# A second home for the first half of each odd expert's w1 in a streamed mixture of experts

## The reference

```python
def _moe(h, w_router, b_router, w1, b1, w2, b2):
    logits = (xt @ w_router + b_router).astype(jnp.float32)
    top_val, top_idx = lax.top_k(logits, TOP_K)            # 4 of 32
    top_w = jax.nn.softmax(top_val, axis=-1)
    gates = ...                                            # 288 x 32, zero where not chosen
    for e in range(N_EXPERTS):
        gu = xt @ w1[e] + b1[e]                            # w1[e]: 1024 x 2048, 8.39 MB
        gate = jnp.minimum(gu[:, :D_FF], SWIGLU_LIMIT)
        up = jnp.clip(gu[:, D_FF:], -SWIGLU_LIMIT, SWIGLU_LIMIT)
        act = (up + 1) * (gate * jax.nn.sigmoid(SWIGLU_ALPHA * gate))
        out = out + gates[:, e:e + 1] * (act @ w2[e] + b2[e])   # w2[e]: 1024 x 1024, 4.19 MB
```

## Time and profile before

| | |
|---|---|
| median of 3 runs | 1116.15 us |
| the profiled execution | 1115.64 us, its span 1113.7 us |
| PE busy | 1053.9 us, 95% of the span |
| DVE, ACT, POOL busy | 393.3, 238.8, 15.5 us |
| DMA | 421.78 MB, mean 379 GB/s over the span |
| mean granted TensorE clock | 0.99 |

### The profile page before, as it was taken

The page is one execution under the profiler, slowest core; times in us unless marked ns, Lnnn a source line. Parts: engine busy times, 40 slices in busy tenths (PEclk is TensorE's granted clock), DMA queues, the critical chain, the costliest instruction groups (busy, mean ns, idle before and its releaser), DMA issues.

```text
span 1113.7 us, 14012 instructions
## 1 busy us (share of the span) xinstructions
PE 1053.9 (95%) x5312; PEld 434.0 (39%) x5313; DVE 393.3 (35%) x694; ACT 238.8 (21%) x473; POOL 15.5 (1%) x27
## 2 busy tenths in 40 slices
PE   8989999999999998999999999999999999999996
PEld 7766454333333333333333333333333333333332
DVE  7683347333333332333333323322322232223326
ACT  3233214221111121222222222111221222111212
POOL 1003000000000000000000000000000000000000
PEclk9989899999999999999999999999999999999998
DMA  9750235999999999999999999999999999999992
GB/s 319 280 227 1 86 155 210 430 428 430 427 430 428 429 428 434 433 432 432 433 433 432 433 432 430 432 431 430 432 431 433 432 433 432 433 425 429 428 428 88
DMA packets 28554, 421.78 MB, mean 379 GB/s; under 512 B 5326, under 2 KB 5966, under 8 KB 11547
## 3 DMA queue, kind: packets, MB, share of 16 engines
q1 hardware_dynamic: 28346, 420.93, 89.4%
q10 hardware_dynamic: 192, 0.66, 0.2%
HBM read 420.11 MB, written 1.46 MB: 379 GB/s over the span
## 4 chain that ended last, share of the span: by engine, by line
PE 51%; DMA 40%; DVE 7%; ACT 1%; issue 1%; SPq 0%; DVEq 0%; ACTq 0%
DMA ring<-in_w_dram 39%; PE ps L880 27%; PE ps L906 8%; PE ps L610 4%; PE ps L727 3%; PE ps L943 1%; DVE area L1598 1%; PE ps L861 1%; PE ps L589 1%; DVE area L1576 1%; DVE area L1572 1%; DVE area L1579 1%; DVE area L1573 1%; PE ps L674 1%; PE ps L872 1%
## 5 line engine op out<-in xcount | busy, mean ns | idle before, releaser
L880 PE MATMUL ps<-ring,area 128*64 128x512 f32 x2048 | 458.1, 597 | 20.3 <-DMA ring<-in_w_dram 20.3
L880 PEld LDWEIGHTS ps<-ring,area 128*64 128x64 f32 x2048 | 142.5, 137 | 291.1 <-issue 245.0
L906 PE MATMUL ps<-ring,area 128*64 128x512 f32 x992 | 224.9, 595 | 0.0
L1598 DVE TENSOR_TENSOR area<-area,ps 128x1024 f32<-128x1024 f32 (+1 forms) x96 | 116.5, 1214 | 55.4 <-PE ps L943 55.4
L1572 DVE TENSOR_SCALAR area<-ps 128x512 f32<-128x512 f32 x31 | 21.4, 692 | 278.5 <-PE ps L880 278.5
L906 PEld LDWEIGHTS ps<-ring,area 128*64 128x64 f32 x992 | 67.5, 136 | 120.7 <-issue 118.3
L1220 ACT ACTIVATE area<-area 128x512 f32<-128x512 f32 x31 | 19.5, 629 | 411.1 <-DVE area L1572 411.1
L1564 DVE SCALAR_TENSOR_TENSOR y_sb<-ps,gcol,y_sb 64x512 fp32r<-64x512 f32 x62 | 46.5, 750 | 98.5 <-ACT y_sb L1182 98.0
L943 PE MATMUL ps<-y_sb,giveT 128*128 128x512 f32 x192 | 69.4, 443 | 11.9 <-DVE area L1598 11.9
L852 PE MATMUL ps<-area 128*64 128x512 bf16 x558 | 66.1, 382 | 0.0
L1182 ACT ACTIVATE y_sb<-ps,gcol 64x512 fp32r<-64x512 f32 x62 | 42.4, 683 | 92.4 <-PE ps L906 91.6
(11 more groups left out here) (238 smaller groups left out, 647.4 us busy)
## 6 DMA issues: line engine op xcount, KB each, us to landing
ring<-in_w_dram SPq DMA_DIRECT2D x60, 4096.0 KB, 20.1
ring<-in_w_dram SPq DMA_DIRECT2D x72, 2048.0 KB, 16.2
area<-in_w_o_dram SPq DMA_DIRECT2D x1, 4096.0 KB, 13.3
area<-in_w_in_dram SPq DMA_DIRECT2D x1, 2560.0 KB, 16.3
area<-in_w_in_dram SPq DMA_DIRECT2D x1, 2336.0 KB, 9.5
area<-in_w_in_dram SPq DMA_DIRECT2D x1, 2048.0 KB, 20.5
lnb<-in_ln_g_dram SPq DMA_DIRECT2D x3, 512.0 KB, 10.4
lnb<-in_ln_b_dram SPq DMA_DIRECT2D x3, 512.0 KB, 11.7
```

The costliest lines, as they stand in the source:

```text
L880: last = mm(ps_gu[g * BLK:(g + 1) * BLK, c, :], x[:, spot(k), :], half_of(w, c, g), start=False, stop=(k == KT - 1))
L906: last = mm(ps_y[g * BLK:(g + 1) * BLK, :], hT[:, c, h, :], w2_t[:, h, c, g * 512:(g + 1) * 512], start=False, stop=(h == 1 and c == 3))
L1598: v.tensor_tensor(acc, acc, src[0:n, :, :], ALU.add).then_inc(done, 1)
```

## The change

The first half of w1 (slots 0 and 1) gets a second home, `late`, two slots wide. Even passes use the ring's slots 0 and 1, odd passes use `late`. The rest of an expert (slots 2 to 5) stays in the ring. To make room, tensors of attention and routing that are dead by then lie inside `late`; those that still live while it fills (`chosen`, `shifted`, `n_more` and so on) move to the end of `area`; `gx` lies on `g_sb`; ln2's gain and bias lie on `rows`, which are free once the rows have been split, so these two loads go out after the first eight passes' loads. PE's loop runs over two passes. SP issues in the order in which buffers come free: the first half of pass p + 2, then the rest of pass p + 1. The table `passes` now holds the first 32 passes as constants, and DVE counts only the further ones, rounded to an even number of passes.

```diff
@@ tensors @@
-        tokT = sb("tokT", [P, KT, TOK])
-        lnb = sb("lnb", [P, 2, D])
-        uext = sb("uext", [P, 4, UW])
+        late = sb("late", [P, 2 * SLOT])
...
+        uext = carve(late, 4 * UW).rearrange("p (g n) -> p g n", g=4)
+        attT = carve(late, 4 * TOK).rearrange("p (k t) -> p k t", k=4)
+        lnb = carve(late, 2 * D).rearrange("p (i n) -> p i n", i=2)
+        assert used[0] >= SLOT
+        tokT = carve(late, KT * TOK).rearrange("p (k t) -> p k t", k=KT)
...
+        gx = g_sb
+        last_giveT = rows[:, 0, 0:TOKP]
+        last_y = rows[:, 0, TOKP:TOKP + D // 2]
+        ln2 = rows[:, 1:3, :]
@@ SyncE @@
             sp.wait_ge(ln_done, 2 * NT)
-            sp.dma_start(lnb[:, 0, :], ln2_g[0].partition_broadcast(P)).then_inc(ln_in[2], 16)
-            sp.dma_start(lnb[:, 1, :], ln2_b[0].partition_broadcast(P)).then_inc(ln_in[2], 16)
...
+            sp.dma_start(late[:, 0:SLOT], w1_part(1, 0)).then_inc(w_in_odd[0], 16)
+            sp.wait_ge(router_ps, 2)
+            sp.dma_start(late[:, SLOT:2 * SLOT], w1_part(1, 1)).then_inc(w_in_odd[1], 16)
+
+            def first_half(i, e, odd, wide):
+
+                base, ready, free = (late[:, :], w_in_odd, odd_free) if odd else \
+                    (ring[:, 0:2, :].rearrange("p s n -> p (s n)"), w_in_slot, slot_free)
+                if wide:
+                    sp.wait_ge(free[0], i + 1)
+                    sp.wait_ge(free[1], i + 1)
+                    sp.dma_start(base, w1_v[col(e), 0].rearrange("e p n -> p (e n)")).then_inc(ready[0], 16)
+                    return
...
+            def two_passes(i, wide):
+
+                even = expert_of(sp, 2 * i + 2)
+                first_half(i, even, False, wide)
+                rest(2 * i + 1, expert_of(sp, 2 * i + 1), wide)
+                first_half(i, expert_of(sp, 2 * i + 3), True, wide)
+                rest(2 * i + 2, even, wide)
+
+            end_wide = last_wide(sp)
+            with sp.Fori(0, WIDE_PAIR) as i:
+                two_passes(i, False)
+            sp.wait_ge(split_ready, NT)
+            sp.dma_start(ln2[:, 0, :], ln2_g[0].partition_broadcast(P)).then_inc(ln_in[2], 16)
+            sp.dma_start(ln2[:, 1, :], ln2_b[0].partition_broadcast(P)).then_inc(ln_in[2], 16)
+            with sp.Fori(WIDE_PAIR, end_wide) as i:
+                two_passes(i, True)
+            two_passes(end_wide, False)
+            rest(2 * end_wide + 3, expert_of(sp, 2 * end_wide + 3), False)
@@ TensorE @@
-                    if k % 2 == 0:
+                    if k % 2 == 0 and k < 4:
+                        pe.wait_ge((w_in_odd if odd else w_in_slot)[k // 2], 16 * (i + 1))
+                    elif k % 2 == 0:
                         pe.wait_ge(w_in_slot[k // 2], 16 * (e + 1))
...
-            with pe.Fori(0, end) as e:
-                expert(e)
+            with pe.Fori(0, end_wide + 1) as i:
+                expert(2 * i, i, False)
+                expert(2 * i + 1, i, True)
+            expert(2 * end_wide + 2, end_wide + 1, False)
@@ ScalarE @@
                 act.wait_ge(x_rows, e + 1)
+                act.wait_ge(sig_ready, e + 1)
+                act.wait_ge(prod_ready, e + 1)
                 copy(gx, ps[:, 2, :]).then_inc(gx_ready, 1)
```

More of the change, by code:

```diff
@@ L35 @@
 TAKEN = -3.0e38
+ROUND = 8388608.0
 BLK = 64
@@ L145, in encoder_kernel @@
         assert BP + 3 * F // 2 + D <= KT * IN
+        flat = area[:, BP + 3 * F // 2:BP + 3 * F // 2 + D]
+        shifted, kept, expo, weighed = (flat[:, i * NT * NE:(i + 1) * NT * NE].rearrange("p (t e) -> p t e", t=NT)
+                                        for i in range(4))
+        n_more, incl, earlier_of = (flat[:, (4 * NT + i) * NE:(4 * NT + i + 1) * NE] for i in range(3))
+        chosen = flat[:, (4 * NT + 3) * NE:(5 * NT + 3) * NE].rearrange("p (t e) -> p t e", t=NT)
         used = [0]
@@ L234, in encoder_kernel @@
         w_in_slot = [sem(f"w_slot{s}") for s in range(NSLOT)]
+        w_in_odd = [sem(f"w_odd{s}") for s in range(2)]
+        odd_free = [sem(f"odd_free{s}") for s in range(2)]
         bias_in = sem("bias_in")
@@ new lines, in _ @@
+            sp.wait_ge(router_ps, 2)
[8 more added lines that the diff above has]
+                    return
+                for s in range(2):
+                    sp.wait_ge(free[s], i + 1)
+                    sp.dma_start(base[:, s * SLOT:(s + 1) * SLOT], w1_part(col(e), s).rearrange("e p n -> p (e n)"))\
+                        .then_inc(ready[s], 16)
@@ new lines, in rest @@
+            def rest(p, e, wide):
+                for s in (2, 4) if wide else (2, 3, 4, 5):
+                    if wide:
+                        src = w1_v[col(e), 1] if s == 2 else w2_whole[col(e)]
+                        dst = ring[:, s:s + 2, :]
+                        sp.wait_ge(slot_free[s + 1], p)
+                    else:
+                        src = w1_part(col(e), s) if s < 4 else w2_v[col(e), s - 4]
+                        dst = ring[:, s, :]
+                    sp.wait_ge(slot_free[s], p)
+                    sp.dma_start(dst, src.rearrange("e p n -> p (e n)")).then_inc(w_in_slot[s], 16)
@@ L556, in _ @@
             pool.wait_ge(ln_in[2], 32)
[L557 to L560, removed]
+            with pool.Fori(WIDE_PAIR, last_wide(pool)) as i:
+                for first, p in ((w_in_slot, 2 * i + 1), (w_in_odd, 2 * i + 2)):
+                    pool.wait_ge(first[0], 16 * (i + 2))
+                    pool.sem_inc(first[1], 16)
+                    for s in (2, 4):
+                        pool.wait_ge(w_in_slot[s], 16 * (p + 1))
+                        pool.sem_inc(w_in_slot[s + 1], 16)
             pool.wait_ge(scaled, 1)
-            nc.gpsimd.tensor_tensor(out_acc[:, 0, :], out_acc[:, 0, :], lnb[:, 1, :], ALU.add).then_inc(result[0], 1)
+            nc.gpsimd.tensor_tensor(out_acc[:, 0, :], out_acc[:, 0, :], ln2[:, 1, :], ALU.add).then_inc(result[0], 1)
         @block.tensor
@@ L882, in up_products @@
                     if k % 2 == 1 and k < KT - 1:
-                        last.then_inc(slot_free[k // 2], 1)
+                        last.then_inc((odd_free if odd and k < 4 else slot_free)[k // 2], 1)
                     if k == 1:
@@ L954, in _, with expert @@
             pe.wait_ge(bias_ready, 1)
-            def expert(e, last=False):
+            def expert(e, i, odd, last=False):
                 pe.wait_ge(xT_ready, e + 1)
                 pe.wait_ge(sel_ready, e + 1)
-                up_products(xT, e)
+                up_products(xT, e, i, odd)
                 if last:
@@ L1026, in add_last @@
                 last.then_inc(sum_ps[t], 1)
-            expert(end, last=True)
+            expert(2 * end_wide + 3, end_wide + 1, True, last=True)
         @block.scalar
@@ L1659, in _ @@
             dve.wait_ge(scaled, 2)
-            v.tensor_tensor(halves(out_acc[:, 1, :]), ps_sum[1], halves(lnb[:, 1, :]), ALU.add).then_inc(result[1], 1)
+            v.tensor_tensor(halves(out_acc[:, 1, :]), ps_sum[1], halves(ln2[:, 1, :]), ALU.add).then_inc(result[1], 1)
             centre(2)
@@ L1664, in _ @@
             dve.wait_ge(norm_ready, NT + 3)
-            v.scalar_tensor_tensor(row, row, rstd[0:TS, 2:3], lnb[0:TS, 1, :], ALU.mult, ALU.add).then_inc(result[2], 1)
+            v.scalar_tensor_tensor(row, row, rstd[0:TS, 2:3], ln2[0:TS, 1, :], ALU.mult, ALU.add).then_inc(result[2], 1)
 _INS = ['x_prompt', 'x_sample', 'cache_k', 'cache_v', 'cache_kidx', 'state_pool', 'ln0_g', 'ln0_b', 'w_in', 'w_o',
```

97 lines of the change are left out of this document (41 added, 56 removed).

## The result

The changed kernel takes 1117.53 us, median of 17 runs (1116.05 to 1119.95), beside 1115.86 for the kernel before in as many runs. The ratio is 1.0018, its 95% interval 1.001 to 1.0025: slower by 1.7 us, clear of no change by the interval, but under the 2.2 us that the prediction took as the line to slower. The forecast was 1118.0. The profiled execution took 1117.42 us with a span of 1115.5, 1.8 longer than before.

A forecast was written before the change was run, and what follows sets the result against it. The weight stream was taken as the bound until pass 28's second half of w1 lands, then TensorE's own pace. 1115.64 + 3.34 - 1.60 + 0.15 = 1117.53, at the median 1118.0 us; own range 1117.0 to 1118.7, overall 1112 to 1123.5.

The forecast's parts named there:

- the line to slower: Verdict threshold: about 0.2%, 2.2 us, from no change, so a time above 1118.4 would count as slower.
- What bounds the end: Last passes: landing of pass 28's second half of w1, plus TensorE's own work from there, plus 1.60 us.
- R28: Pass 28's loads of slots 2 to 5; their half was forecast to land near 995.8, before just ahead of 992.39.
- The prefetch frees only pass 31's waits: Stream's end: only pass 31's loads come 9.7 us earlier, removing its waits of 1.07 and 0.53, gain 1.60 us.
- The ln2 loads: Two loads moved behind pass 8's weights: delay later second halves and the end by 3.34 us (bounds 2.4 and 3.4).
- The doubled loop: TensorE's loop body over two passes: some 570 instructions, three or four 16 KB packets, priced at nothing in the sum.
- The routing arithmetic: VectorE's extra tiny operations before pass_cols, ready about 175.2 instead of 174.47: +0.15 us (bounds 0 and 0.7).
- Pass 9: TensorE waits about 5.8 us instead of 2.14, perhaps with a longer low clock, hidden by 1.18 us a pass.
- (1): Weight stream: the whole 9.7 us of the prefetch come through, 1109.9 us; chance 0.14.
- (2): ln2 loads in the stream: cost nothing visible, as the same 4 KB is read 128 times, 1114.7 us; chance 0.10.
- (3): Wide part of the stream: runs at the narrow part's rate, 428 not 432, adding 5.4 us, 1123.4; chance 0.08.
- (4): Doubled TensorE loop: instructions fetched at each turn, about 1134 to 1138, taken as 1136 us; chance 0.06.

The follow-up runs named there:

- The experiment that takes the lead out ahead of R: Changed kernel with ln2 loads last and, from pass 9, slots 2 to 5 of the next pass loaded before the following pass's first half; ratio to before 0.9944.
- plain rows: Changed kernel with ln2 loads after all weights, plus two 512 KB loads of different w1 rows in their old place behind pass 8's loads; ratio to before 1.0020.
- the loop of five: Kernel before with only TensorE's loop written over five passes (6 turns); ratio to before 1.0001.
- the experiments on ln2: Changed kernel, ln2 loads after all weights: 0.9999; the same plus a plain megabyte in the stream: 1.0020; kernel before, only ln2 loads moved into the stream: 1.0019.
- the three points tried here: Changed kernel, ln2 loads last, slots 2 to 5 loaded ahead of the following first half from pass 9, 17 or 25; ratios to before 0.9944, 0.9970, 0.9957.
- the loop of two: Kernel before with only TensorE's loop written over two passes (15 turns, then pass 30 and the last); ratio to before 1.0002.

## Why the prediction was right, and where not

**What bounds the end: right.** The end is R28's landing plus TensorE's own work. The change moved R28 by 3.82 us and, from the same start, the end by 1.92; before and after, passes 29 to 31 start 27.96 apart.

**The prefetch frees only pass 31's waits: right.** Predicted 1.60. Measured: R28 +3.82 and the end +1.92, so 1.90. The 0.3 above the prediction lie in pass 31, which takes 24.33 us from its first matmuls to its last 16 before and 22.44 after: the two waits held it up by 1.9 us, not only by the 1.60 of idle time that the rows show. The experiment that takes the lead out ahead of R shows the rest of the 9.7 us: it was in the buffer and unused.

**The ln2 loads: right in kind, the size off.** Predicted 3.34 with 2.43 as the lower bound; measured 2.4 to 2.7, counted from load 12, and 2.5 for plain rows: the lower bound was the right price. The term of the sum that was mis-sized is "a further load costs its engine time, and I take 3.34".

**The doubled loop: the term that was missing.** I treated the packets only as a question of refetching at each turn, which does not occur, and took none for the first turn. They, or something else in the doubled body, set the stream back by 1.2 us in the first profile of the changed kernel and by 0.5 in the second. That the loop is the cause is shown by the kernel of before with this edit alone, twice; that a packet holds up one of the engines is my reading, and the loop of five speaks against the plain form of it. By luck this term, the error in ln2's and the one in pass 31's nearly cancel: 2.6 + 1.2 - 1.9 = 1.9 in the first profile against 3.34 - 1.60 + 0.15 = 1.89, and 1.7 in the medians. In the second profile the end moved by 1.2 only.

**The routing arithmetic: right.** The chain from the first comparison to pass_cols takes 2.89 us where it took 2.22, and is still ready 0.59 before TensorE asks. The first pass starts 0.12 earlier than before, well within the scatter of starts.

**Pass 9: right in kind.** 6.50 us of wait against 5.8 forecast, and a longer stretch at a lower granted clock (10.00 for 7.11 us of matmuls), hidden as forecast: TensorE waits for the stream again from pass 12 on.

**The rivals.** The whole 9.7 us (1) did not come through, and ln2's loads were not free (2): the experiments on ln2 show both. The stream is not slower in its wide part (3): it runs at 432 GB/s, 29.15 us a turn. TensorE does not fetch at each turn (4): no q8 packet is there from the second turn to the last.

## What to carry to other kernels

Before adding a buffer to a stream that is already full, count the bytes that stand ahead of each load that is waited for. A prefetch that is kept ahead for good, because the order of issue refills it at once, makes no waited load earlier; it must be spent at a point, by taking one load out from ahead of the others. Of the three points tried here the earliest was the best, by the end of the profiles. And put side loads where the stream has a hole or behind its end: in the middle of it they cost their bytes in full.

## What the hardware showed that I had not expected

Writing TensorE's loop over two passes instead of one delays every later load by about 1 us (0.3 to 2.2 by load 12, in ten profiles), from the fifth of the stream on, though no wait of TensorE for its instructions shows; with five passes it is 0.8. What in the longer body does it is not shown.

The spread of starts (175.5 to 179.5 us over the fourteen profiles) means that a difference of a few us between single times says less than one position counted from a common mark, and a second mark further on can tell two causes apart that the first lumps together. TensorE's store held a loop of five passes, over six turns, with seven packets of 16 KB in all.

The length of a wait alone does not give its price in clock. A wait of 2.14 us in pass 9 was followed by 32 matmuls in 8.79 us in the kernel before, and in the second profile of the loop of two by the same 32 in 7.09:

```profile
439.45 7.09 PE L880 MATMUL ps<-ring,area 128*64 128x512 f32 x32 [2.14 <-DMA ring<-in_w_dram]
```
